# Gate and up blocks of an FFN multiplied pairwise in seven half products

## The reference

```python
hn = rmsnorm_2(h, ffn_norm_g)
ff = jax.nn.silu(jnp.einsum('bld,df->blf', hn, w_gate)) * jnp.einsum('bld,df->blf', hn, w_up)
return h + jnp.einsum('blf,fd->bld', ff, w_down)
```

## Time and profile before

| what | value |
|---|---|
| median of 3 runs | 3331.46 us (3329.18 to 3336.09) |
| profiled execution: span | 3326.5 us (runs' median is 5.0 us above it) |
| PE busy | 3110.3 us, 94% of the span |
| DVE busy | 1787.3 us, 54% |
| ACT busy | 1176.6 us, 35% |
| POOL busy | 299.1 us, 9% |
| matmul instructions | 19072 |
| second network, first layer's FFN | 2195.7 to 2569.7 us |
| second network, last layer's FFN | 2949.5 to 3308.9 us |

### The profile page before, as it was taken

One profiled execution on the slowest core, in us unless ns is written; L12 is line 12 of the kernel. 1 busy time (PEld: TensorE's weight loads), 2 busy tenths in 40 slices (PEclk: granted clock), 3 DMA queues, 4 the chain that ended last, 5 costly groups with the idle time before them and its releaser, 6 DMA issues. The chain is left out here.

```text
span 3326.5 us, 49141 instructions
## 1 busy us (share of the span) xinstructions
PE 3110.3 (94%) x19072; PEld 2726.2 (82%) x19072; DVE 1787.3 (54%) x2840; ACT 1176.6 (35%) x1843; POOL 299.1 (9%) x268
## 2 busy tenths in 40 slices
PE   3999889999997999899999999999999999899998
PEld 2678877888886687789987897899999898778886
DVE  8558677465565567554443545554344345554444
ACT  3243534232232443544444332343223332243222
POOL 1000210101102001112223000010001000010001
PEclk8999889999998998899999999999999999999999
DMA  7231033232332231122222111122323211122322
GB/s 265 74 111 60 12 114 121 95 126 101 107 116 95 68 116 45 46 84 93 93 90 89 57 46 45 52 89 83 107 84 101 71 45 51 51 93 84 107 88 95
DMA packets 105693, 288.68 MB, mean 87 GB/s; under 512 B 36272, under 2 KB 36400, under 8 KB 104272
## 3 DMA queue, kind: packets, MB, share of 16 engines
q1 hardware_dynamic: 100304, 269.73, 24.3%
q0 software_dynamic: 3808, 10.38, 0.9%
q10 hardware_dynamic: 1440, 6.62, 0.5%
HBM read 284.56 MB, written 2.10 MB: 86 GB/s over the span
## 5 line engine op out<-in xcount | busy, mean ns | idle before, releaser
L343 PE MATMUL ps<-h_hi,hi_ring 128*128 128x512 f32 (+2 forms) x2672 | 872.3, 326 | 64.5 <-DVE h_lo L716 41.3
L270 DVE TENSOR_TENSOR lo_ring<-ring,hi_ring 128x1024 fp32r<-128x1024 f32 (+1 forms) x410 | 484.6, 1182 | 700.9 <-ACT hi_ring L260 696.6
L343 PE MATMUL ps<-h_lo,hi_ring 128*128 128x512 f32 (+2 forms) x2672 | 843.5, 316 | 0.0
L343 PE MATMUL ps<-h_hi,lo_ring 128*128 128x512 f32 (+2 forms) x2672 | 840.5, 315 | 0.0
L260 ACT ACTIVATE hi_ring<-ring 128x1024 fp32r<-128x1024 f32 (+1 forms) x410 | 420.1, 1025 | 1032.2 <-PE ps L343 992.0
L343 PEld LDWEIGHTS ps<-h_hi,hi_ring 128*128 128x128 f32 x2672 | 513.9, 192 | 126.5 <-issue 81.8
L343 PEld LDWEIGHTS ps<-h_lo,hi_ring 128*128 128x128 f32 x2672 | 515.1, 193 | 33.6 <-issue 3.9
L343 PEld LDWEIGHTS ps<-h_hi,lo_ring 128*128 128x128 f32 x2672 | 512.5, 192 | 30.9
L343 PE MATMUL ps<-ffn_operand,hi_ring 128*128 128x264 f32 (+1 forms) x2112 | 479.7, 322 | 1.5 <-DVE lo_ring L270 1.5
L343 PEld LDWEIGHTS ps<-ffn_operand,hi_ring 128*128 128x128 f32 x2112 | 350.5, 188 | 35.1 <-issue 1.8
L343 PE MATMUL ps<-ffn_operand,lo_ring 128*128 128x264 f32 (+1 forms) x1056 | 339.1, 321 | 0.0
(11 more groups left out here) (360 smaller groups left out, 3842.6 us busy)
## 6 DMA issues: line engine op xcount, KB each, us to landing
ring<-weights_dram SPq DMA_DIRECT2D x334, 512.0 KB, 3.3
mod_ring<-w_mod_dram SPq DMA_DIRECT2D x64, 512.0 KB, 4.2
ring<-weights_dram SPq DMA_DIRECT2D x76, 384.0 KB, 3.0
arena<-w_mod_dram SPq DMA_DIRECT2D x48, 512.0 KB, 3.4
x<-x_dram SPq DMA_DIRECT2D x1, 3072.0 KB, 16.6
arena<-c_rows_dram ACTq DMA_DIRECT2D x3, 1024.0 KB, 6.6
arena<-ret_decay_dram POOLq DMA_DIRECT2D x2, 1056.0 KB, 6.0
silu_rows<-c_rows_dram ACTq DMA_DIRECT2D x2, 1024.0 KB, 5.3
```

Of the source, the lines that this page charges most:

```text
L270: self.nc.vector.tensor_tensor(self.lo_ring[:, g % SPLIT, 0:w], self.ring[:, g % RING, 0:w], self.hi_ring[:, g % SPLIT, 0:w], ALU.subtract ...
L343: ins = nc.tensor.matmul(out[0:m, c:c + n], w, a[:, t0:t0 + n], start=first and k == 0 and p == 0, stop=last and k == kts - 1 and p == 2)
```

## The change

With G1, G2 and U1, U2 the upper and lower halves (in K) of a gate and an up block, and the operand cut into halves of K and of tokens, the 2 x 2 x 2 block product is formed in seven products in place of eight, each of 4 tiles of K and half the tokens (264 or 256 columns). Some multiply raw halves, the others sums.

- POOL makes four sums of 128 x 512 per pair (`add_weights`).
- ACT and DVE split seven operands of 128 x 512 (`part_hi`, `part_lo` of `SevenProducts`) in place of two blocks of 128 x 1024. Three have slots of their own (`seven_operands`), four use the halves of the two slots of `hi_ring` and `lo_ring`. Each has one slot, so it is refilled when its product in the pair before is done.
- PE makes seven products in four PSUM banks of 264 or 256 columns; the fifth, sixth and seventh accumulate into banks that hold the first, fourth and third, after these have been read. Pairs alternate between two sets of four banks.
- DVE combines them with six reads of PSUM (after a copy of the first by ACT), then goes on as before, with one buffer each for gate, sigmoid and up where there were two. The up part and with it the hidden operand are no longer times 1/rms; the down products are, by one more DVE instruction each.
- In the output projection's loop ACT and DVE make the token and feature sums of `ffn_operand`, some in `h_hi` and `h_lo`.
- Many semaphores get shared names; the order is not changed by that.

The core of the diff:

```diff
+    def add_weights(self, pool, t, n, p):
+        self.landed(pool, t, p, 0)
+        self.landed(pool, t, p, 1)
...
+        if n:
+            pool.wait_ge(self.lo.sem, t * 10 + self.lo.at(5 * (n - 1) + 2))
+        tt(sums[:, 0, :], ring(1, 0), ring(1, 1), ALU.add).then_inc(self.made.sem, 1)
+        made(1)
...
+        tt(sums[:, 1, :], sums[:, 0, :], ring(0, 0), ALU.add).then_inc(self.made.sem, 1)
...
+        tt(sums[:, 2, :], ring(0, 0), ring(1, 0), ALU.add).then_inc(self.made.sem, 1)
+        if n:
+            pool.wait_ge(self.core.lo, t * 4 + (self.g0 + 2 * p if p else self.g0 - 2 * KT))
+        tt(sums[:, 3, :], sums[:, 1, :], ring(0, 1), ALU.add).then_inc(self.made.sem, 1)
...
+    def multiply(self, pe, t, n, p, q, acts, before=None):
+        if q < 5:
+            pe.wait_ge(self.lo.sem, t * 10 + self.lo.at(5 * n + q + 1))
...
+        if q >= 4:
+            pe.wait_ge(self.taken.sem, t * 2 * EVACUATIONS + self.taken.at(EVACUATIONS * n + q - 3))
+        out = self.bank(p, (0, 2, 1, 3, 0, 3, 2)[q])
...
-                def pair(t, i):
-                    core.part_hi(act, t, b0 + 2 * i + SPLIT)
...
+                def pair(t, i, final=False):
+                    following = lambda q: seven.part_hi(act, t, n0 + i + 1, i + 1, q)
+                    seven.came(act, t, n0 + i, i, 0)
+                    nc.scalar.activation(taken[:, 2, 0:width], seven.bank(i, 0), ACT.Copy).then_inc(seven.copied.sem, 1)
+                    for q in range(0 if final else 6):
+                        following(q)
+                    act.wait_ge(taken_in.sem, t * 2 + taken_in.at(n0 + i + 1))
+                    nc.scalar.activation(sig_f[:, 0:tokens], gate_f[:, 0:tokens], ACT.Sigmoid).then_inc(sigmoid.sem, 1)
...
+                        following(6)
                     act.wait_ge(product_ready.sem, t * 2 + product_ready.at(n0 + i + 1))
...
+                    following(0)
+                    following(1)
+                    seven.came(dve, t, n, i, 2)
+                    dve.wait_ge(seven.copied.sem, t * 2 + seven.copied.at(n + 1))
+                    took(v.tensor_tensor(second, seven.bank(i, 1), taken[:, 2, 0:width], ALU.subtract))
+                    following(2)
+                    seven.came(dve, t, n, i, 3)
+                    own(1)
+                    took(v.tensor_tensor(third, seven.bank(i, 3), second, ALU.add))
+                    following(3)
+                    own(2)
+                    took(v.tensor_tensor(u2, third, seven.bank(i, 2), ALU.subtract))
+                    if start:
+                        inverse_norm()
+                    seven.came(dve, t, n, i, 4)
+                    took(v.tensor_tensor(g1, seven.bank(i, 0), r1, ALU.mult))
+                    following(4)
+                    seven.came(dve, t, n, i, 5)
+                    took(v.tensor_tensor(u1, seven.bank(i, 3), second, ALU.add))
+                    following(5)
+                    seven.came(dve, t, n, i, 6)
+                    took(v.tensor_tensor(g2, seven.bank(i, 2), second, ALU.subtract))
+                    own(6)
+                    v.tensor_tensor(g2, g2, r2, ALU.mult).then_inc(taken_in.sem, 1)
+                    following(6)
...
+                        v.tensor_tensor(like_psum(out_sum[:, 0:tokens], tokens), in_psum(core.buf(f0 + o), tokens),
+                                        like_psum(r, tokens), ALU.mult).then_inc(scaled.sem, 1)
+                        dve.wait_ge(scaled.sem, t * 2 + scaled.at(side * KT + o + 1))
+                        v.tensor_tensor(x_out, out_sum[:, 0:tokens], x_out, ALU.add).then_inc(core.free.sem, 1)
```

More of the change, by code:

```diff
@@ L2408, in hybrid_layer @@
     n_out, n_up, n_down = MIX_BLOCKS, 2 * H_TILES, 2 * KT
-    outs = n_up + KT
+    outs = KT
+    t_made, taken_in = core.counter("operand_sums_made"), core.counter("gate_ready_in_sbuf")
+    scaled = core.counter("output_scaled")
+    sides = [SevenProducts(core, extra, w_sums, core.block0 + MIX_BLOCKS + OUT_BLOCKS + side * (n_up + n_down), width)
+             for side in range(HALVES)]
     ffn_gain = lambda k: core.param[:, P_FNORM + l * KT + k:P_FNORM + l * KT + k + 1]
@@ L2680, in _, with up, operand_ready @@
                 b0, f0 = MIX_BLOCKS + OUT_BLOCKS + side * (n_up + n_down), MIX_BLOCKS + OUT_BLOCKS + side * outs
[L2682 to L2687, removed]
+                seven, n0 = sides[side], side * H_TILES
+                def up(t, i, at=0, before=None):
+                    for q in range(7):
+                        seven.multiply(pe, t, n0 + at + i, at + i, q, seven_acts, before)
+                        if before is not None and q == 3:
+                            pe.wait_ge(core.added.sem, core.added.at(KT))
+                            product(nc, acc, [core.ones[:]], [core.sumsq[:]], tokens, P).then_inc(f_summed.sem, 1)
+                def operand_ready(q, k):
+                    n = (2 * k + 1, 2 * k + 2, KT + 4 * k + 1, KT + 4 * k + 2, KT + 4 * k + 3, KT + 4 * k + 4,
+                         KT + 4 * k + 3)[q]
+                    pe.wait_ge(g_ready.sem, g_ready.at(n))
                 def down(t, i):
@@ L2897, in _ @@
                     for i in range(UNROLL):
-                        out((n_down - UNROLL) // UNROLL, i)
+                        out((n_down - UNROLL) // UNROLL, i, True)
         @block.vector
@@ L3146, in _, with first_operands @@
             col_steps.close(col.n)
+            def first_operands(side, i, last_block):
+                for q in ((0, 1, 2), (3, 4), (5, 6))[i - last_block + 2] if i >= last_block - 2 else ():
+                    sides[side].part_lo(dve, 0, side * H_TILES, 0, q)
             for i in range(OUT_BLOCKS):
@@ new lines, in _, with pair, following @@
+                n0, seven = side * H_TILES, sides[side]
+                def pair(t, i, final=False, start=False):
+                    n = n0 + i
+                    g, sg, u = gate_f[:, 0:tokens], sig_f[:, 0:tokens], up_f[:, 0:tokens]
+                    (g1, g2), (u1, u2) = halves(g), halves(u)
+                    second, third = taken[:, 0, 0:width], taken[:, 1, 0:width]
+                    at = lambda m: t * 2 * EVACUATIONS + seven.taken.at(EVACUATIONS * n + m)
+                    own = lambda m: dve.wait_ge(seven.taken.sem, at(m))
+                    took = lambda ins: ins.then_inc(seven.taken.sem, 1)
+                    def following(q):
+                        if not final:
+                            seven.part_lo(dve, t, n + 1, i + 1, q)
+                    following(0)
[23 more added lines that the diff above has]
+                    following(6)
+                    if final:
+                        for m in range(SPLIT):
+                            core.part_lo(dve, 0, b0 + n_up + m)
+                    dve.wait_ge(sigmoid.sem, t * 2 + sigmoid.at(n + 1))
+                    v.tensor_tensor(sg, sg, g, ALU.mult).then_inc(gated.sem, 1)
+                    dve.wait_ge(gated.sem, t * 2 + gated.at(n + 1))
+                    v.tensor_tensor(u, u, sg, ALU.mult).then_inc(product_ready.sem, 1)
+                    dve.wait_ge(hid_done.sem, t * 2 + hid_done.at(n + 1))
```

312 lines of the change are left out of this document (233 added, 79 removed).

## The result

| | before | after |
|---|---|---|
| median, us | 3330.3 (3328.6 to 3336.1, 4 runs) | 3518.9 (3512.5 to 3530.5, 4 runs) |
| ratio | | 1.0565, 95% interval 1.0543 to 1.0588 |
| profiled span, us | 3326.5 | 3518.9 |
| PE busy, matmuls | 3110.3, 19072 | 3138.5, 19600 |
| DVE busy, instructions | 1787.3, 2840 | 2119.6, 3378 |

(The matmul count rises because the last layer's 48 of 512 columns became 84 of 256 per pair; in the layer before 96 became 84.) The change costs 192 us of span (189 between the medians). The forecast was 3475, 144 above the time that it started from: direction and mechanism came out, 48 us of the size did not.

A forecast was written before the change was run, and what follows sets the result against it. PE-bound before; after, DVE, taking turns with POOL at SBUF, bounds pairs at 14.5 us. Four sides' +138.6 and smaller terms make +144 on 3331.5: 3475 us, range 3360 to 3530; main case (chance 0.52) 3430 to 3520.

The forecast's parts named there:

- PE stays bound: Pair loops: chain shorter than 5.84 us, port waits fall into DVE's idle time, 61 us gained less 10 to 15: 3280; chance 0.10.
- First reason: Pair loops: the chain through in-order queues stalls PE 1.7 us, period 11.95 us (11.68 before), last layer 11.75 against 11.23.
- The rival of 3381 (chain only): Pair loops: no port waits of weight, periods 11.95 and 11.75, +45 and 5 for small terms: 3381 us; chance 0.20.
- POOL is slower: Pair loops: POOL additions of 1.5 us and more, or PSUM reads that wait as well: 3507 us; chance 0.15.
- Second reason: Pair loops: POOL and DVE take turns at SBUF, DVE waits 3.4 us a pair, its round is 14.5 us.
- Clock, nothing booked: Whole kernel: a stretch with PE idle 10 of 120 us keeps 0.96, nothing booked, a few us possible.
- Table loads +6.4: First sides: of two table loads per two pairs, the one ahead of ACT's copy is on the chain, 5 x 1.28 = 6.4 us.
- First pair of a side: Start of a second side: the first pair finds operands and sums made, and PE runs 4.3 us faster.
- Last two pairs 1.2 us faster: End of a second side: last two pairs together 1.2 us faster, though the first down block waits for two subtractions.
- Gate and up in sum: Gate-and-up stages: second sides +26.4 and +29.9 us, first sides +39.4 and +42.9; these four +138.6.
- Output projection +2 per layer: Output projection: 3 to 4 more short ACT and DVE instructions per block, 2 us booked per layer (0 to 6).
- Down stages and ends +1.5: Down stages: scaled read and addition hidden under products of 8 us, but 0.75 on the path at each layer's end: 1.5.

The follow-up runs named there:

- e4_order_no_sums: Changed kernel without GpSimd's additions, ScalarE's copy and VectorE's subtraction for the next pair moved ahead of the hidden tile's rounding and rest: 3362.8 us, ratio 1.0097.
- the first two experiments: Changed kernel with GpSimd's four additions per pair left out: 3435.2 us; changed kernel with these additions half as wide: 3474.9 us.
- e1_no_sums: Changed kernel with GpSimd's four additions per pair left out, four products taking raw quarters of the weights instead: 3435.2 us, ratio 1.0318.

## Why the prediction was right, and where it was short

| kernel | total, us | pair of the second side, us | of these at full clock |
|---|---|---|---|
| before | 3330 | 11.68 | all |
| after | 3519 | 14.7 | 14.7 |
| half-width additions | 3475 | 12.6 to 14.2 | 12.6 |
| no additions | 3435 | 12.2 to 13.7 | 12.2 |
| no additions, waits filled | 3401 | 12.2 | 12.2 |
| order | 3467 | 13.6 to 13.7 | 13.65 |
| order, no additions | 3363 | 11.3 | 11.3 |

- *PE's work falls 61 us; DVE, not PE, sets the pair.* Right. The rival "PE stays bound" falls: PE waits in every pair. Without additions PE is busy for 10.4 of 12.2 us in a pair at full clock. The result lies at the edge of the main case's own range (3430 to 3520), since 48 us were missing.
- *First reason, a chain of 11.95 us through the in-order queues.* Right: 12.2 at full clock with the additions out. That it is order and not work is shown by e4_order_no_sums: the same instructions in another order take 11.3. The rival of 3381 (chain only) needed the additions to be free; they are not. The rival "POOL is slower" named 3507, nearer to 3519 than the forecast, but not by what happened: three of a pair's additions take 1.27 to 1.30 us, only the fourth 1.69, and the PSUM reads do not wait.
- *Second reason, turns at SBUF.* Right in mechanism and size: 3.5 us of waits against 3.4, removed with the additions, shrunk with their width; when DVE does the additions itself the total is the same.
- *Clock, nothing booked.* Right in the pair loops, for a reason that was not given: DVE and POOL are the chain. In the expectations of the first two experiments, where PE came back onto the chain, it was a wrong term. In the changed kernel it failed (the prediction allowed "a few us") where PE is the bound, at the start of each down stage. There PE has waited 3.4 to 3.6 us for the first block's rest (first line: the wait ahead of layer 0's second down stage), and its first 3.4 us run at half clock: 16 matmuls (second line, after) where there were 30 (third line, before).

```profile
2595.14 0.51 PE L343 MATMUL ps<-hidden,hi_ring 128*128 128x264 f32 x2 [3.39 <-DVE lo_ring L270]
...
2368.02:2371.42 3.40, 3.40 (x16) 3.40 (x17) 2.63 (x4) 0.64 (x1) 0.00 (x0) 0.53 0.61 192
...
2312.62:2316.02 3.40, 3.40 (x30) 3.40 (x29) 2.90 (x4) 1.49 (x2) 0.00 (x0) 1.00 0.02 5
```

  That is 1.6 us in each of the four, 6.4 in all.
- *Table loads +6.4, the period of 15.8 in every second pair.* Right: every second pair takes 16.0 us, and moving the loads took off 12 us for both layers (12.8 booked).
- *First pair of a side: PE runs 4.3 us faster.* This step failed. From a second side's first matmul to the end of its first pair's seventh product the step gives 10.2 us in layer 0 (14.5 less 4.3) and 9.9 in the last, PE's bare work. It took 13.8 in both (first line, after, layer 0); without additions it takes 10.2 and 9.9, to a tenth what the step had (second line, e1_no_sums):

```profile
2433.78:2447.60 13.82, 11.96 (x86) 11.77 (x85) 11.91 (x15) 5.22 (x9) 9.35 (x7) 0.88 0.22 78
...
2408.14:2418.34 10.20, 10.20 (x87) 10.20 (x86) 8.57 (x15) 5.24 (x9) 0.00 (x0) 1.00 0.33 104
```

  The working had the first pair's operands and sums ready and overlooked what stands in the queues just then: POOL makes the sums of pair 0 and of pair 1 nearly back to back, beside the last subtractions of the stage before and the first of the next pair. DVE's timeline at the start of layer 0's second side:

```profile
2429.29 1.78 DVE L2380 TENSOR_TENSOR seven_operands<-ring,seven_operands 128x512 fp32r<-128x512 f32 x1
...
2435.34 1.78 DVE L2380 TENSOR_TENSOR lo_ring<-ring,hi_ring 128x512 fp32r<-128x512 f32 x1
2437.05 1.78 DVE L2380 TENSOR_TENSOR lo_ring<-arena,hi_ring 128x512 fp32r<-128x512 f32 x1
2438.76 0.68 DVE L2380 TENSOR_TENSOR seven_operands<-ring,seven_operands 128x512 fp32r<-128x512 f32 x1
2439.36 1.76 DVE L2380 TENSOR_TENSOR seven_operands<-arena,seven_operands 128x512 fp32r<-128x512 f32 x1
```

  "Second" comes at 2441.04 behind them. PE waits 1.9 us, until 2441.61, and a fall of the clock behind the wait costs the other 1.7.
- *Last two pairs 1.2 us faster, the wait of the first down block included.* This failed too. From the ninth pair's end to the first down matmul the forecast has 27.9 us in layer 0's second side, and it took 29.9: behind the last product stand DVE's g2 and its product with 1/rms, ACT's sigmoid and rounding of the down block, and DVE's rest, before PE goes on.
- *Gate and up in sum.* In layer 0's second side the first pair is 3.6 over, the second 0.1, the seven in the middle 0.9 and the end 2.0: the 6.5 by which that side exceeded its term. The other three exceeded theirs by 5.3 to 8.6, 26 us in all; in a first side of layer 0 the first pair takes 19.7 where the terms give 17.6 (10.2 + 5.0 + 2.4), and two pairs of 15.6 at clock 0.78 are in the last side.
- *Output projection +2 per layer (0 to 6).* This term was mis-sized: +8.1 in both layers, outside its own bounds. It counted DVE's instructions by their unhindered lengths and left out the second reason, which works there as well. In layer 0 PE's waits for DVE's rests grow from 2.5 to 7.9 us; the remaining 2.7 come with a granted clock of 0.87 in place of 0.92.
- *Down stages and ends +1.5.* Right for what it counted: from a layer's last down matmul to the next product 5.21 us became 5.95, and 4.64 became 5.36. The down stages' other 6.4 us are the clock's, above. The last 3.5 us lie outside these stages, where the changed kernel's twelve variants scatter from 2.5 less to 4.7 more than before; no cause is to be read from them.

12 (projections) + 26 (gate and up) + 6 (clock in the down stages) + 3.5 (scatter) are the 48 us that were missing.

## What to carry to other kernels

Sum up an engine's new work not only by its durations but by who else reads SBUF at that moment: a GpSimd addition cost VectorE nearly its own length, as much as if VectorE had done it. Work out the chain through the in-order queues for a steady iteration, and then once more for the first iteration and for the stage ahead of it, where preparation for the loop piles up, and for its end: most of the 48 us that this forecast lacked lie there. A wait at such a seam can cost twice, since the clock may be at half behind it. And cutting a bound engine's work by 12% is worth nothing until the engine that feeds it has slack at the one instruction that frees the buffer; a new order of the same instructions was worth 103 us here, more than the 61 that the removed matmuls could have given.

## What the runs showed of the hardware beyond that

- GpSimd loses turns as well. In the output projection one addition (L2335) stood behind three DVE instructions issued back to back, and took 3.28 us in place of 1.29; its squares' additions took 3.04 and 3.02 us where 1.8 was usual. POOL was kept off through several queued DVE instructions, while POOL's own back-to-back additions let one DVE instruction in between each (the 1.78 us rows above). Two of POOL's groups in that stage:

```profile
L2335 POOL TENSOR_TENSOR arena<-ring 128x512 f32<-128x512 f32 x1 | 3.3, 3282 | 2.5 <-DMA ring<-weights_dram 2.5
...
L2343 POOL TENSOR_TENSOR arena<-ring 128x512 f32<-128x512 f32 x1 | 1.4, 1365 | 0.1
```

- With one wait of 1.8 us in every pair the granted clock was 0.88 in most of them, and matmuls that nobody reads kept it at 1.00 and made the kernel 34 us faster. Where PE was not on the chain, pairs at 0.88 and at 1.00 lasted the same 14.7 us.
